# Hybrid decoder layer on one core: GpSimd's operations of 1024 columns made as two of 512

## The reference

```
mod = silu(c) @ w_ada + b_ada                     # six rows: shift, scale, gate, twice
h   = x * (1 + sc1) + sh1
proj = h @ w_in                                   # 1024 -> 2048: b, c, x | u, v | pool
y_a = b * conv3(c * x)                            # 256 channels
y_b = u * (W_s @ LN(v) + b_s)                     # 512 channels, chunks of 128 positions
y_c = (trailing means of 2/4/8/16 - p) @ pool_w * pool_scale   # 256 channels
x   = LN(alpha * x + g1 * ([y_a, y_b, y_c] @ w_out))
h2  = x * (1 + sc2) + sh2
x   = LN(alpha * x + g2 * (relu(h2 @ w_up)^2 @ w_down))        # 4096 hidden channels
```

## Time and profile before

| | |
|---|---|
| median of 3 runs | 2261.89 us |
| profiled execution | 2263.62 us, its span 2261.9 us |
| TensorE busy | 94% of the span, mean granted clock 0.973 |
| VectorE busy | 73% |
| GpSimd busy | 58%, 445 low parts with a mean of 2573 ns |
| ScalarE busy | 38% |
| DMA | 357.75 MB, 158 GB/s on average |

### The profile page before, as it was taken

The page is one execution under the profiler, slowest core; times in us unless marked ns, Lnnn a source line. Parts: engine busy times, 40 slices in busy tenths (PEclk is TensorE's granted clock), DMA queues, the critical chain, the costliest instruction groups (busy, mean ns, idle before and its releaser), DMA issues.

```text
span 2261.9 us, 27348 instructions
## 1 busy us (share of the span) xinstructions
PE 2136.4 (94%) x10342; PEld 1761.7 (78%) x10342; DVE 1657.6 (73%) x2068; ACT 861.3 (38%) x1172; POOL 1316.5 (58%) x650
## 2 busy tenths in 40 slices
PE   7989999999989999999989999989999989999985
PEld 4556787887889788888768888778888789999974
DVE  1555589688587776588789878699868687666788
ACT  1201322323212355445544445544444534444430
POOL 3323476774323356667666776677666655565664
PEclk9999999999989999999999999999999989999997
DMA  8546687794423354544534654524564433453331
GB/s 258 163 143 225 202 244 230 216 285 144 126 90 100 94 191 142 181 155 158 159 102 140 213 187 144 172 83 152 185 214 134 161 93 122 135 193 124 123 102 42
DMA packets 324085, 357.75 MB, mean 158 GB/s; under 512 B 16280, under 2 KB 256105, under 8 KB 323954
## 3 DMA queue, kind: packets, MB, share of 16 engines
q1 hardware_dynamic: 323954, 355.99, 49.9%
HBM read 321.34 MB, written 34.59 MB: 157 GB/s over the span
## 4 chain that ended last, share of the span: by engine, by line
PE 56%; DVE 12%; ACT 1%; issue 1%; POOL 0%; DVEq 0%; ACTq 0%
PE ps L1066 18%; PE ps L1067 18%; PE ps L1068 18%; PE ps L1330 1%; DVE hid_a L1853 1%; DVE hid_b L1853 1%; DVE xt L1895 1%; DVE pair_sums L1874 1%; DVE pair_sums L1871 1%; DVE acc L1965 1%; DVE acc L1966 1%; DVE acc L1959 1%; DVE pair_sums L1872 1%; DVE pair_sums L1873 0%; DVE acc L1948 0%
## 5 line engine op out<-in xcount | busy, mean ns | idle before, releaser
L845 POOL TENSOR_TENSOR w_hilo<-w_raw,w_hilo 128x1024 fp32r<-128x1024 f32 x445 | 1139.7, 2573 | 885.6 <-ACT w_hilo L920 884.5
L920 ACT ACTIVATE w_hilo<-w_raw 128x1024 fp32r<-128x1024 f32 x445 | 469.7, 1057 | 734.6 <-PE ps L1068 641.8
L1066 PE MATMUL ps<-hA,w_hilo 128*128 128x512 f32 (+1 forms) x1760 | 630.0, 358 | 29.1 <-ACT htmp L973 9.3
L1067 PE MATMUL ps<-hA,w_hilo 128*128 128x512 f32 (+1 forms) x1760 | 627.0, 356 | 0.0
L1068 PE MATMUL ps<-hA,w_hilo 128*128 128x512 f32 (+1 forms) x1760 | 626.3, 356 | 0.0
L1066 PEld LDWEIGHTS ps<-hA,w_hilo 128*128 128x128 f32 x1760 | 337.3, 192 | 75.0 <-issue 21.4
L1067 PEld LDWEIGHTS ps<-hA,w_hilo 128*128 128x128 f32 x1760 | 337.7, 192 | 42.6
L1068 PEld LDWEIGHTS ps<-hA,w_hilo 128*128 128x128 f32 x1760 | 337.0, 191 | 42.5
L1948 DVE TENSOR_TENSOR acc<-acc,ps 128x512 f32<-128x512 f32 x270 | 178.3, 685 | 81.5 <-PE ps L1068 78.6
L1066 PE MATMUL ps<-w_hilo,hid_a 128*128 128x512 f32 x450 | 179.4, 399 | 19.0 <-DVE acc L1948 16.3
L1067 PE MATMUL ps<-w_hilo,hid_a 128*128 128x512 f32 x450 | 176.9, 393 | 0.0
(11 more groups left out here) (233 smaller groups left out, 3098.8 us busy)
## 6 DMA issues: line engine op xcount, KB each, us to landing
w_raw<-in_w_up SPq DMA_DIRECT2D x128, 512.0 KB, 4.0
w_raw<-w_mix SPq DMA_DIRECT2D x124, 512.0 KB, 3.3
w_raw<-in_w_down SPq DMA_DIRECT2D x97, 512.0 KB, 3.7
w_raw<-in_w_in SPq DMA_DIRECT2D x64, 512.0 KB, 4.7
xt<-in_w_ada SPq DMA_DIRECT2D x22, 1024.0 KB
w_raw<-in_w_out SPq DMA_DIRECT2D x32, 512.0 KB, 5.2
xt<-x_norm SPq DMA_DIRECT2D x19, 512.0 KB, 5.8
xt<-in_w_down SPq DMA_DIRECT2D x36, 256.0 KB, 5.3
```

Source lines behind the costliest of these rows:

```text
L845: pool.tensor_tensor(W[:, g % SLOTS, 1, :], raw[:, g % RAW, :], W[:, g % SLOTS, 0, :], ALU.subtract).then_inc(lo_done, 1)
L920: act.activation(W[:, g % SLOTS, 0, :], raw[:, g % RAW, :], ACT.Copy).then_inc(hi_done, 1)
L1066: pe.matmul(out, w_hi, x_hi, start=start, stop=False)
L1067: pe.matmul(out, w_hi, x_lo, start=False, stop=False)
```

## The change

Both operations of GpSimd that take 1024 columns inside the flow of slabs are issued as two of 512 columns, one after the other. The wait stands ahead of the first, the semaphore is counted up by the second. `HALF` is 512.

```diff
--- before.py
+++ after.py
@@ -842,8 +842,11 @@
 
             def lo_part(g):
                 pool.wait_ge(hi_done, g + 1)
-                pool.tensor_tensor(W[:, g % SLOTS, 1, :], raw[:, g % RAW, :], W[:, g % SLOTS, 0, :],
-                                   ALU.subtract).then_inc(lo_done, 1)
+                for half in range(2):
+                    cols = slice(HALF * half, HALF * half + HALF)
+                    ins = pool.tensor_tensor(W[:, g % SLOTS, 1, cols], raw[:, g % RAW, cols],
+                                             W[:, g % SLOTS, 0, cols], ALU.subtract)
+                ins.then_inc(lo_done, 1)
 
             lo_part(0)
             lo_part(1)
@@ -865,8 +868,11 @@
 
             def gate_acc(s, t):
                 pool.wait_ge(sums_ready, 2 * s + (1 if t >= 2 else 2))
-                a = acc[:, t, :]
-                pool.tensor_tensor(a, a, rows[:, G2_ROW, :], ALU.mult).then_inc(acc_gated, 1)
+                for half in range(2):
+                    cols = slice(HALF * half, HALF * half + HALF)
+                    a = acc[:, t, cols]
+                    ins = pool.tensor_tensor(a, a, rows[:, G2_ROW, cols], ALU.mult)
+                ins.then_inc(acc_gated, 1)
 
             def weight_mix(c, buf):
```

## The result

The changed kernel took 2242.47 us (median of 4 runs, 2240.41 to 2247.82), the kernel before 2261.23 on the same chip: a ratio of 0.9917, 95% interval 0.9896 to 0.9938, so some 19 us or 0.8% faster. The forecast was 2249 and -13 us.

The account below looks back on a forecast made before the run. TensorE, busy 94% of the span, was taken as the bound, so only its waits count. Terms of -5.4, -2.3, -1.0, -3.0, -1.9, -2.5 and +3.1 sum to -13.0 us: 2249 us, range 2241 to 2264.

Parts of the forecast that it names:

- first mixer: TensorE's 1.03 us gap at 130.35: one VectorE operation behind one low part comes 1.05 us earlier, -1.0 us.
- pool maps of mixers 1 and 2, with their clock: Two 4.17 us gaps: awaited VectorE results 2.7 us earlier each, -5.4 us, plus half the slow-clock cost, -2.3 us.
- block before a group's end: Waits of about 3.77 us in three groups: VectorE's `L1874` ends earlier behind a half, three times 1.0, -3.0 us.
- group ends 0 to 2: Bursts of low parts and gatings: first costs 0.2 us, second lets VectorE through earlier; net -0.9, -0.9, -0.7, together -2.5 us.
- last block: Gap at 2161.91: VectorE passes four turns of 1.2 us in place of three of 2.25, -1.9 us.
- end of the kernel: Waits at 2206.35 and 2211.83: VectorE's turns between halves delay the low parts TensorE awaits, net +3.1 us.
- rival 1: Between halves of a pair: the port isn't passed to VectorE, each hit costs 0.2 us more, +8.8 us, 2270.7 us; 10%.
- Rival 2: Rows of down slabs within blocks: GpSimd becomes late and TensorE waits for low parts, 2277 us; 5%.
- Price of a pair: Everywhere on GpSimd: two halves cost 0.2 us more than one whole; a half's turn in a burst is 1.2 us.
- Rival 3: At the shortened gaps: another releaser stands behind each, so earlier results are hidden, 2260 to 2263 us; 18%.
- elsewhere TensorE doesn't stand: All places not listed, such as the last mixer's pool sums: an earlier VectorE gives nothing, 0 us.
- a shorter wait may well spare it: Behind the pool-map gaps: TensorE's half-clock stretch, some 2.4 and 2.2 us, may vanish; half taken, -2.3 us.

Follow-up runs that it names:

- e6: Changed kernel, but low parts and gatings as two pieces of 256 and 768 columns, the short one first: 2236.27 us, 0.9870 of the kernel before.
- e7: Changed kernel, but low parts and gatings as two pieces of 768 and 256 columns, the long one first: 2251.56 us, 0.9933 of the kernel before.
- e8: Changed kernel with a semaphore wait between the two halves of each pair: 2242.08 us, 0.9897 of the kernel before.
- e1: Kernel before with only the low parts in halves, the 16 gatings whole: 2249.10 us, 0.9930 of the kernel before.
- e4: Changed kernel, but the last four low parts and last four gatings whole: 2239.03 us (median of three runs), 0.9892 of the kernel before.
- e5: Kernel before with halves only for the low parts of the mixers' slabs, MLP low parts and gatings whole: 2258.45 us, 0.9968 of the kernel before.
- e2: Kernel before with only the 16 gatings in halves, the low parts whole: 2257.14 us, 0.9972 of the kernel before.
- e3: Changed kernel, but low parts and gatings as four pieces of 256 columns everywhere: 2218.22 us, 0.9796 of the kernel before.

## Why the prediction was right

The direction and the range hold, and so does the mechanism: VectorE gets a turn after each half. But the largest term of the sum failed, two places that were put at nothing gave 5.3 us, and one was four times its forecast. That the total came within 6.5 us of the runs is partly luck. In microseconds, measured as in the table of parts:

| place | forecast | measured |
|---|---|---|
| first mixer | -1.0 | -0.5 in its wait (-1.2 with the loads) |
| pool maps of mixers 1 and 2, with their clock | -7.7 | -0.2 (both mixers) |
| last mixer | 0 | -4.1 |
| blocks 0 to 6 | 0 | -1.2 |
| block before a group's end | -3.0 | -2.7 |
| group ends 0 to 2 | -2.5 | -10.1 |
| last block | -1.9 | -2.1 |
| end of the kernel | +3.1 | +0.3 |
| sum | -13.0 | -21.3 |

With the pool maps as forecast and the rest as measured it would have been some 29 us and outside the range; the measured 2242.47 us lies 1.5 us above its lower end.

- *VectorE is let in between the halves* (against rival 1): right, shown by 1.40 us in the burst and by e6 against e7. Rival 1 is out. e8 shows that the missing wait never mattered. Rival 2 is out for halves: TensorE has no wait for a low part between 830 and 1080 us.
- *Price of a pair*: free 2.55 us against 2.4, as estimated. In a burst I took 1.2 us for a turn, it is 1.11. At eight halves a burst that is 0.7 us each time, in place of the "+0.2" at the first burst of a group's end.
- *Pool maps*: 5.4 us and half of the clock's cost, -7.7 in all. The waits vanished as worked out (`L1520` ended at 367.97, 5.1 us earlier beyond the shift of 1.2, more than the upper end of 3.2), but the step from there failed: that TensorE didn't stand again for 100 us behind 374.33 was true of the trace of before, and it did stand once it came earlier. The trace of before could have told, by the stretch ahead of the gap (columns as in the earlier trace rows, the third busy time is VectorE's, 13.04 of 13.30 us; that includes time in which it stands):

```profile
361.00:374.30 13.30, 9.16 (x41) 7.26 (x39) 13.04 (x8) 2.12 (x2) 12.18 (x8) 0.96 0.76 217
```

  VectorE went on like that up to the products with w_out, whose input it makes. Before, this input was ready only 0.77 us before TensorE came for it, at 388.82 for 389.59:

```profile
387.71 1.11 DVE L1514 TENSOR_TENSOR mix<-acc,mix 128x512 fp32r<-128x512 f32 x1
...
389.59 0.47 PE L1066 MATMUL ps<-w_hilo,mix 128*128 128x512 f32 x1
```

  In the changed kernel it was ready at 385.73, 1.9 us earlier beyond the shift of 1.2. TensorE, rid of a wait of 4.17 us and of a slow stretch, came 7.9 us earlier, at 381.69, and stood. So no more than 2.7 us could be kept there. The rows of the changed kernel:

```profile
366.40 0.43 DVE L1519 CAST spl<-htmp 128x512 fp32r<-128x512 f32 x1
...
366.86 1.11 DVE L1520 TENSOR_TENSOR spl<-htmp,spl 128x512 fp32r<-128x512 f32 x1
...
381.29 1.64 DVE L1520 TENSOR_TENSOR mix<-acc,mix 128x512 fp32r<-128x512 f32 x1
...
384.63 1.09 DVE L1520 TENSOR_TENSOR mix<-acc,mix 128x512 fp32r<-128x512 f32 x1
```

  Mixers 1 and 2 gave 0.2 us in all. With halves there too, e1 lost 1.8 us and e4, e5 and e8 gained 0.9, 0.9 and 2.8: nothing near 7.7. Rival 3 held here, for this term.
- *Last mixer*: put at nothing, under "elsewhere TensorE doesn't stand". But TensorE did stand there, 1.06 and 2.03 us for `DVE acc`, with a granted clock of 0.72 on average behind the second:

```profile
689.00:695.00 6.00, 4.21 (x20) 4.21 (x21) 5.76 (x8) 0.13 (x1) 2.96 (x1) 0.72 0.24 73
```

  Short VectorE operations behind a whole low part were in the way. The first addition of 176 columns took 2.43 us before and 0.34 after:

```profile
669.01 2.43 DVE L1690 TENSOR_TENSOR acc<-acc 128x176 f32<-128x176 f32 x1
```

```profile
666.24 0.34 DVE L1696 TENSOR_TENSOR acc<-acc 128x176 f32<-128x176 f32 x1
```

  The second half did hit other operations of the row, as told, but less was paid for them than was won, and this stretch gave 4.1 us in each of the runs with halves in the mixers (e1, e4, e5, e8 too). It is the steadiest gain of the change. The wait at 828.70 (blocks 0 to 6) was left out in the same way: 0.95 us and 1.2 with what follows, in e1, e4 and e8 as in the changed kernel, and nothing in e2 and e5, where these low parts are whole.
- *Clock*: the stretch behind the pool map at 0.50 went, and the new wait brought one of its own. TensorE's granted clock before and behind it in the changed kernel (columns as in the earlier trace rows):

```profile
385.80:389.50 3.70, 3.63 (x9) 2.91 (x10) 3.63 (x3) 0.00 (x0) 3.16 (x3) 0.54 0.69 148
...
366.00:372.00 6.00, 6.00 (x28) 4.95 (x27) 5.79 (x7) 1.06 (x1) 5.84 (x6) 1.00 0.67 171
```

  The step "a shorter wait may well spare it" didn't hold: behind 3.77 us at 1092.05 the granted clock had stayed at 1.00, and behind the 2.83 us in its place it was 0.50 from 1086 to 1089. At the next group it was the other way round (0.50 behind 1438.26 before, 1.00 behind 1428.16 after), and at the third it fell in both. That makes the +0.6, -2.5 and -0.8 of the table.
- *Block before a group's end*: 0.94 to 0.95 us of each wait, as worked out, and the three slow stretches more or less cancel. *Last block*: 2.1 against 1.9.
- *Group ends*: -10.1 in place of -2.5, the term that was mis-sized. TensorE's waits make 6.0 of it (2.8, 1.8 and 1.4), most at the waits for ScalarE's `htmp`, and shorter stretches at half clock the rest, which I hadn't counted. One part is the turn of 1.11, by an estimate 0.7 us for each burst of eight halves. Another may be that I added the bursts up and didn't follow ScalarE. How much that makes was not tried by itself.
- *End of the kernel*: +3.1 forecast, +0.3 measured, by the table and by e4. The wait for the low part grew as told (2188.71), but by 3.9 us where I had 5 to 5.6; twelve turns of 1.11 in place of 1.2 are 1.1 of the difference. VectorE's `hid_b` was off the path, and the slow stretch behind it (granted clock 0.50 from 2213.3 to 2216.3) went with it, about 1.7 us. I had counted the cost of the one wait and not the whole of what the other gave back.
- *First mixer*: the wait of 1.03 us became 0.53, half of what I took. In the shift it can't be told from the start-up, which varies by more.

## What to carry to other kernels

Where VectorE and GpSimd both read SBUF, look at the longest GpSimd operation that a short VectorE operation on the path can meet, and cut that, as long as GpSimd's free time for a whole round of work stays below what the consumer needs: here 2.4, 2.55, 2.95 and 3.8 us a slab for one, two, four and eight pieces, so 26, 28, 32 and 42 us a block of eleven slabs, against 41. The first piece matters (e6 against e7), and the ones behind it too: quarters are another 0.7% ahead of e6, whose first piece is as short. Before a gain is booked at a wait, ask whether the waited-for engine is free until the next meeting; if it works without a pause, the wait only moves. And before a place is put at nothing, list its waits: here 4 us stood in three small ones. Quarters with a whole end are the best version found, 0.9774 of the time before, though its interval overlaps that of quarters everywhere.

## What the runs showed of the hardware

- A piece's turn in a burst is 2.2, 1.11 and 0.55 us for 1024, 512 and 256 columns: in proportion to its columns, while alone it takes 2.4, 1.27 and 0.74, with about 0.2 us fixed (0.47 for 128 columns fits this). The turns are estimates: the fourth pair sum or its like took 2.50, 1.40 and 0.84 us beside such pieces (kernel before, changed kernel, e3), less 0.29 of its own. No fixed part is seen in them.
- Two orders of the same two pieces (e6, e7) lie 15 us apart in a kernel of 2250.
- Equal waits of TensorE didn't have equal effects on its clock: behind 2.81 us at 1428.16 none, behind 2.56 us at 1474.68 a stretch with a mean of 0.60. Shorter waits at the block before a group's end, 1.57 us in e6 and 1.85 in e3, had a granted clock of 1.00 behind them at all three groups. The rows of the first two:

```profile
1428.00:1434.00 6.00, 5.84 (x28) 4.85 (x29) 3.95 (x7) 2.48 (x4) 4.27 (x4) 1.00 0.53 175
...
1474.70:1479.00 4.30, 4.30 (x12) 3.42 (x13) 3.19 (x3) 4.03 (x6) 2.33 (x2) 0.60 0.33 98
```
